# A two-block transformer step on one core: five context tiles put between the second mixer's attention steps, and the memory attention taken in halves

## The reference, cut to what matters

```python
def first_block(x, mem, ...):                     # DEPTH = 2
    mem_n = rmsnorm(mem, mem_norm)
    for i in range(DEPTH):
        h = rmsnorm(x, mix_norm[i])
        ...                                       # memory K and V from mem_n: 4 heads of 64
        # i == 0: gated short convolution; i == 1: stick-breaking attention, 12 heads,
        #         on k_sh, v_sh = kv of rmsnorm(x, kv_norm), taken after layer 0
        y_mem = memory_cross_attention(q_mem, mem_k, mem_v)
        x = x + jnp.concatenate([y_main, y_mem], axis=-1) @ w_o[i]
        x = x + swiglu(rmsnorm(x, ffn_norm[i]), w_gate[i], w_up[i], w_down[i])   # 1024 -> 2816 -> 1024
        ...
    return rmsnorm(x, final_norm)

def _context_states(hc, w_in, gla_w2, gla_b2, s0):
    k, v, lr = _split(hc @ w_in[:, OFF_KVG:], IN_SPLITS[6:])
    _, s_f, s_b = _gla_bidir(None, ..., lr, gla_w2, gla_b2, s0, s0)
    return s_f, s_b

# second_block: modulations = silu(c) @ w_ada + b_ada, and the same of c_ctx
hc = _modulate(_rms_norm(ctx, norm1_g[l]), sh1c, sc1c)
s_f, s_b = _context_states(hc, ...)               # lr 1 tile, k 4 tiles, v 8 tiles of weights
hx = _modulate(_rms_norm(x, norm1_g[l]), sh1x, sc1x)
y_x, _, _ = _token_mixer(hx, *tm, s_f, s_b)       # then a convolutional feed-forward and a last norm
```

## Time and profile before

| | |
|---|---|
| runs | 1208.05, 1209.74, 1212.25 us; median 1209.74 |
| the profiled execution | 1211.49 us; its span 1210.2 us |
| granted TensorE clock over the span | 0.984 |
| PE busy | 1157.9 us (96%) |
| DVE, ACT, POOL busy | 833.1, 622.6, 149.4 us |
| HBM read | 219.42 MB |

### The profile page before, as it was taken

How to read it: one execution, slowest core, us unless ns; L and a number is a source line. 1 busy time by engine, 2 the same in 40 slices (tenths; PEclk the granted TensorE clock), 3 DMA queues, 4 the chain that set the end, 5 groups by cost and what they waited for, 6 DMA issues and landing times.

```text
span 1210.2 us, 21837 instructions
## 1 busy us (share of the span) xinstructions
PE 1157.9 (96%) x9014; PEld 1110.4 (92%) x9014; DVE 833.1 (69%) x1278; ACT 622.6 (51%) x938; POOL 149.4 (12%) x111
## 2 busy tenths in 40 slices
PE   7999999999899899999999999999999989999996
PEld 6999999999788789999998898979899988999995
DVE  5677677778774756877787756577646767677775
ACT  5655444445564645444455664656437444555553
POOL 0003000000100012000000000000001032344431
PEclk9999999999999989999999999999999997999999
DMA  8655587776744144877877445354324552556550
GB/s 310 195 163 178 165 295 253 240 246 229 244 128 136 51 157 146 263 263 252 274 265 232 160 157 166 105 174 140 114 95 158 185 182 90 186 178 192 175 157 36
DMA packets 60467, 221.90 MB, mean 183 GB/s; under 512 B 6752, under 2 KB 7008, under 8 KB 59984
## 3 DMA queue, kind: packets, MB, share of 16 engines
q1 hardware_dynamic: 59904, 219.06, 55.0%
q10 hardware_dynamic: 288, 1.05, 0.2%
q0 software_dynamic: 176, 0.39, 0.1%
HBM read 219.42 MB, written 1.05 MB: 182 GB/s over the span
## 4 chain that ended last, share of the span: by engine, by line
PE 81%; DVE 10%; ACT 5%; issue 3%; DMA 1%; SPq 0%; POOL 0%; ACTq 0%; DVEq 0%
PE PS L350 23%; PE PS L352 22%; PE PS L351 22%; PE PS L355 13%; DVE w_lo L1316 4%; ACT w_hi L837 3%; DVE PS L1889 1%; DVE SQ L1587 1%; DMA ARENA<-memT 1%; DVE raw L1338 0%; DVE SQ L1352 0%; DVE ARENA L1352 0%; PE PS L455 0%; DVE H_lo L1362 0%; ACT ARENA L925 0%
## 5 line engine op out<-in xcount | busy, mean ns | idle before, releaser
L1316 DVE TENSOR_TENSOR w_lo<-raw,w_hi 128x1024 fp32r<-128x1024 f32 x325 | 398.8, 1228 | 259.9 <-ACT w_hi L837 259.4
L837 ACT ACTIVATE w_hi<-raw 128x1024 fp32r<-128x1024 f32 x356 | 372.5, 1054 | 141.7 <-PE PS L352 117.4
L350 PE MATMUL PS<-Y_hi,w_hi 128*128 128x256 f32 x1240 | 358.4, 289 | 9.6 <-DVE w_lo L1316 4.2
L351 PE MATMUL PS<-Y_lo,w_hi 128*128 128x256 f32 x1240 | 353.9, 285 | 0.0
L352 PE MATMUL PS<-Y_hi,w_lo 128*128 128x256 f32 x1240 | 353.8, 285 | 0.0
L350 PEld LDWEIGHTS PS<-Y_hi,w_hi 128*128 128x128 f32 x1240 | 240.8, 194 | 16.2 <-issue 9.4
L351 PEld LDWEIGHTS PS<-Y_lo,w_hi 128*128 128x128 f32 x1240 | 241.2, 194 | 0.4 <-issue 0.2
L352 PEld LDWEIGHTS PS<-Y_hi,w_lo 128*128 128x128 f32 x1240 | 241.0, 194 | 0.0
L350 PE MATMUL PS<-H_hi,w_hi 128*128 128x256 f32 x808 | 232.1, 287 | 5.3 <-DVE w_lo L1316 2.8
L351 PE MATMUL PS<-H_lo,w_hi 128*128 128x256 f32 x808 | 229.3, 284 | 0.0
L352 PE MATMUL PS<-H_hi,w_lo 128*128 128x256 f32 x808 | 229.2, 284 | 0.0
(11 more groups left out here) (206 smaller groups left out, 1316.7 us busy)
## 6 DMA issues: line engine op xcount, KB each, us to landing
raw<-stream SPq DMA_DIRECT2D x404, 512.0 KB, 4.2
ARENA<-memT SPq DMA_DIRECT2D x2, 512.0 KB, 7.7
X<-xT SPq DMA_DIRECT2D x1, 1024.0 KB, 11.4
ARENA<-c_rows SPq DMA_DIRECT2D x2, 512.0 KB, 8.2
ARENA<-memT SPq DMA_DIRECT2D x1, 1024.0 KB, 7.1
ARENA<-ctxT SPq DMA_DIRECT2D x1, 1024.0 KB, 8.1
outT<-ARENA SPq DMA_DIRECT2D x2, 512.0 KB, 2.6
CROW<-c_rows SPq DMA_DIRECT2D x1, 512.0 KB, 10.2
```

The source lines that it names most:

```text
L350: pe.matmul(o, wh, xh, start=start, stop=False, skip_group_check=True)
L351: pe.matmul(o, wh, xl, start=False, stop=False, skip_group_check=True)
L837: act.activation(w_hi[n % RING][:], raw[at][:], ACT.Copy).then_inc(*mark("hi", n))
L1316: dve.tensor_tensor(w_lo[n % RING][:], raw[raw_of("slot", n)][:], w_hi[n % RING][:], ALU.subtract).then_inc(*mark("lo_dve", n))
```

## The change

It does six things.

1. `STAGES`: `ctx_lr` and `ctx_k` (five tiles) move from behind `ffn1` to behind `kv_v1`. They read the context's norm from `CX_hi`, `CX_lo`, new names for the places of `CTX` and `CSQ`.
2. The attention of the second mixer: PE scores the memory heads at step 1 of `b_q` instead of step 7; its two halves of heads wait for their own marks; on ACT and DVE it runs interleaved with the norm for K and V (`both`). It ends on all three engines at step 13, and `stick_schedule` starts there on all three. Before, PE started the groups at step 18 and ACT and DVE at 17.
3. `stick_output` becomes `stick_outputs`, a task beside the groups, at steps 14, 16 and 18 of its own count.
4. The context's squares and norm: `context_rms` moves to `a_u`/`a_b`, `context_norm` to the last six j of `ffn0` behind `memory_norm`; its 1 MB load moves with it, to tile `a_c`+4.
5. The 16 double mods lie in j = 0 to 15 of `ffn0`; `ffn1` has 32 single ones (two for odd j from 3 on). The second load and silu of c_ctx go.
6. `block1_end` has 8 tiles beside it instead of 13, with new steps.

```diff
@@ STAGES, MODS_AFTER
-          ("kv_v1", 2), ("w_o1", KC), ("ffn1", FFN_SLOTS),
-          ("ctx_lr", 1), ("ctx_k", 4), ("ctx_v0", 4), ("ctx_v1", 4),
+          ("kv_v1", 2), ("ctx_lr", 1), ("ctx_k", 4), ("w_o1", KC), ("ffn1", FFN_SLOTS),
+          ("ctx_v0", 4), ("ctx_v1", 4),
...
-    if _j % 2 == 0 and _both < CTX_MODS:
-        _now = [_both]
+    if _l == 0:
+        _now = [_j] if _j < CTX_MODS else []
     else:
-        _now = [CTX_MODS + _one + i for i in range(2 if _l and _j in (11, 13, 15, 17) else 1)]
+        _now = [len(MOD_ORDER) + _i for _i in range(2 if _j % 2 and _j > 2 else 1)]
...
+def both(first, second):
+    live = [first, second]
+    while live:
+        live = [task for task in live if next(task, "end") != "end"]
+        if live:
+            yield
...
@@ PE, memory_attention
                 last.then_inc(*mark("ma_scores", l))
-                for b in bs:
-                    emptied[b] = [("ma_exp", l, 7)]
-                yield from nothing(6)
-                pe.wait_ge(*past("ma_prob", l, 7))
-                claim(*bs)
                 for h in range(MEMH):
+                    emptied[bs[h]] = [("ma_exp", l, 2 * h + 1)]
+                for h in range(MEMH):
+                    if h % 2 == 0:
+                        yield from pace.to(7 + l + h // 2)
+                    pe.wait_ge(*past("ma_prob", l, 2 * h + 1))
+                    claim(bs[h])
                     for mt in range(TT):
...
                 for h in range(MEMH):
+                    if h % 2 == 0:
+                        yield from pace.to(9 + l + h // 2)
+                    if h == 0:
+                        claim(*os)
                     pe.wait_ge(*past("ma_pt", l, h))
...
-                yield
+                yield from pace.to(12 + l)
@@ PE, stick_outputs
-            def stick_output():
+            def stick_outputs():
+                pace = Pace()
                 for c in range(MC):
-                    b = 4 + c // 2
+                    b = 2 + c // 2
                     if c % 2 == 0:
+                        yield from pace.to(14 + c)
                         claim(b)
+                    if c == 0:
+                        pe.wait_ge(*past("vs", 1))
                     pe.wait_ge(*past("am", c))
@@ PE, block1_end
+                pace = Pace()
                 yield
                 quarters("final")
-                yield
-                yield
+                yield from pace.to(2)
                 sum_quarters("final")
-                yield
-                yield from nothing(5)
+                yield from pace.to(6)
                 quarters("norm1")
-                yield
-                yield
+                yield from pace.to(7)
                 sum_quarters("norm1")
-                yield from nothing(KC + 2)
@@ PE, order of the stages
-            side.tasks += [memory_attention(1), stick_schedule(stick_group, lambda: kept)]
+            side = Side(memory_attention(1), both(stick_schedule(stick_group, lambda: kept), stick_outputs()))
...
+            project("ctx_lr", 1, CX, lambda i: ("lr", 0), side, [norm_low("ctx", k) for k in range(KC)])
+            project("ctx_k", GH, CX, lambda i: ("kb", 0, i), side)
             side.finish()
-            pe.wait_ge(*past("vs", 1))
-            stick_output()
-            side = Side(context_rms())
...
-            project("w_o1", KC, H, lambda i: ("added", 1, i), side, y_ready)
-            side.finish()
-            ffn(1, Side(nothing(KC + 1)))
+            project("w_o1", KC, H, lambda i: ("added", 1, i), None, y_ready, order=(0, 1, 2, 3, 6, 7, 4, 5))
+            ffn(1)
@@ ACT and DVE, memory_attention(1) beside the norm for K and V
+            side.tasks = [both(memory_attention(1), chain(*side.tasks)),
+                          both(stick_schedule(stick_group, lambda: kept), stick_outputs())]
@@ DVE, memory_attention: maxima and probabilities by halves, at steps 1, 3 and 4
-                dve.tensor_reduce(mx.rearrange("p (h t) -> p h t", h=4), scores, AX,
-                                  ALU.max).then_inc(*mark("ma_max0", l))
...
+                for half in range(2):
+                    hs, cols = slice(2 * half, 2 * half + 2), slice(4 * half, 4 * half + 4)
+                    dve.tensor_reduce(mx[:, cols].rearrange("p (h t) -> p h t", h=2), scores[:, hs], AX,
+                                      ALU.max).then_inc(*mark("ma_max0", l, half))
...
+                for half in range(2):
+                    cols = slice(4 * half, 4 * half + 4)
+                    yield from pace.to(3 + half)
+                    dve.wait_ge(*past("ma_exp", l, 4 * half + 3))
...
@@ DVE, block1_end
+                pace = Pace()
                 add_down(1)
-                yield from nothing(3)
+                yield
+                yield from pace.to(3)
                 dve.wait_ge(*past("rs", "final"))
                 for c in range(KC):
...
-                    if c % 2:
-                        yield
-                yield from nothing(3)
+                    if c == 3:
+                        yield from pace.to(4)
+                yield from pace.to(8)
```

217 lines of the change are left out of this document (99 added, 118 removed).

## The result

The changed kernel takes 1219.92 us in the median of four runs (1218.57 to 1222.87), beside 1210.32 of the kernel before (1208.05 to 1212.25): a ratio of 1.0083 (of the means), with a 95% interval from 1.0057 to 1.0109. It is slower by about 10 us where 1207.5 was forecast, and lies outside the range.

A forecast was written before the change was run, and what follows sets the result against it. PE was taken as the bound, busy 1157.9 of 1210.2 us. Terms -2.9 -3.8 -1.2 -2.7 +6.6 +1.7 = -2.3 took the profiled 1211.5 to 1209.2, about 1207.5 for a median; range 1200.5 to 1214.

The forecast's parts named there:

- the price of the lower clock: Half-clock time after new PE waits of 2 us or more: one new drop net, +1.7 us, between 0 and 5.
- stick groups: Second mixer's attention groups: moved tiles cover part of the chain, new waits remain; -3.8 us, bounds -12.0 and 0.
- memory attention: Memory heads in b_q: earlier scores and halves cut the excess from 5.3 to 2.4 us, so -2.9.
- context's squares: Context's squares and sum, moved earlier: about 2 us of PE in either place, so no change.
- ffn0, ffn1: The feed-forwards with mods and norms rearranged: -1.2 us in the first, -2.7 in the second.
- end of the block: First block's end with eight wide tiles instead of 13: cover taken away, +6.6 us, bounds +0.6 and +8.
- three new long waits: PE waits of 2 us or more: before group 5's tails, the second quarters and inside the lr tile.
- The slower rival: Many short and three long waits bring the lower clock repeatedly: five drops, +6.8 us, 1214.3 us; chance 0.16.
- Sum 8.2: New loss in the attention groups: waits before tails of groups 1 to 5 and z of groups 0 and 1, us.
- old 12.0: Excess in us of the kernel before, from 409.36 to 439.92, the end of w_o1's first tile.
- masks in time: Attention groups: tiles cover the chain, none of the 8.2 us of waits comes back, 1199.3 us; chance 0.12.
- norms in time: First block's end: its two waits (2.9 and 3.2 us) don't show, 1201.4 us; chance 0.12.

The follow-up runs named there:

- halves alone: The kernel before with only the memory attention by halves, scores six steps earlier; groups, tiles, mods and context norm stay where they were: 1207.88 us, ratio 0.9974.
- wait made on purpose: The kernel with the groups and block's end both repaired, plus six POOL operations that PE must await at chunk 6 of lr: 1207.09 us, ratio 0.9962.
- the block's end made sooner: The changed kernel with the steps of the first block's end laid for eight tiles, x_final, squares and norm sooner: 1210.49 us, ratio 0.9994.
- more matmuls: The changed kernel with extra unread matmuls (8, 4, 9 and 18) ahead of four waits between 667 and 702 us: 1217.98 us, ratio 1.0050.
- the repair: The changed kernel with ACT and DVE one step ahead of PE in every attention group, as in the kernel before: 1208.97 us, ratio 0.9978.
- the two repairs: The changed kernel with ACT and DVE one step ahead in the groups and the block's end laid for eight tiles: 1197.25 us, ratio 0.9878.

## Why the prediction was wrong

Two terms of the sum carry most of the miss: the price of the lower clock (+1.7, and +5.5 came) and the gain of the stick groups (-3.8, and -0.6 came). Each line below is a term, as predicted and as the profiled executions show it. They stand for 7.1 of the 9.6 us between the medians: the changed kernel's profiled execution was its fastest, with a granted clock of 0.987 where the other three have 0.983 or 0.984, and no trace shows where those lost more.

| term | predicted | measured | how |
|---|---|---|---|
| memory attention | -2.9 | -2.9 | halves alone: 46.41 to 43.49 |
| stick groups | -3.8 | -0.6 | 122.90 to 117.0 is -5.9; less 2.9 and the 2.4 of the context's squares that left w_o1 (22.51 - 7 x 2.88) |
| ffn0, ffn1 | -1.2, -2.7 | -0.9, -1.4 | 197.14 to 196.22, 193.56 to 192.14; in ffn0 only 0.3 is the change's: the kernel with the halves alone, which lacks the low row at 133.44, has 196.54 |
| context's squares | 0 | +0.7 | a_b 17.28 to 20.39, less the 2.4 |
| end of the block | +6.6 | +7.8 | 30.5 to 38.69, less 0.4 that the clock took in lr (38.30 without) |
| clock | +1.7 | +5.5 | k 3.5, lr 0.4, vs0 1.6 |
| start | 0 | -1.1 | mem_k0 21.30 to 20.19; 19.7 to 21.6 in the experiments, whose edits don't touch it |
| sum | -2.3 | +7.1 | profiled: 1218.57 - 1211.49 = 7.1 |

**The clock, "I take one new drop net: +1.7".** This term is off most, by 3.8 us, though 1.6 of it lies at vs0, where a low stretch comes and goes between kernels. Of the three new long waits two came (2.47 and 2.64); the third was 1.22. And one drop of the clock followed the wait in lr, as forecast. The price was wrong: I took it from a row of 3.41 us at half clock, and the wait in lr was followed by 10.24, or by 6.83 in two experiments; k and lr paid 3.9. The wait made on purpose confirms it from outside: 3.29 us cost 7.6 in lr and k. The slower rival had five drops, 8.5 us in all, brought by the many short waits; what came was 5.5 from two places.

The prediction weighed the Trainium skill there (TensorE: Matmul & The Clock Gate, HAM oscillation and the second failure mode: frequent small idles make the clock swing). The traces do not agree with it here: the crowded stretch 340.62 to 472.03, with all its waits, has a granted clock of 1.00, while one wait of 3.03 us among full tiles brought a low row. They contradict it only in part: in two other kernels with the same steps (the block's end made sooner, more matmuls) a row of 3.41 us at half clock stands behind the wait of 2.5 us ahead of the last tails, at 432 and 433. The same page of the Trainium skill (Why this matters for your kernels) warns of single long pauses between bursts of matmuls, but only of pauses longer than this one. The traces agree that a single wait can do it, and not with that limit: 10.24 us at half clock followed 2.64 us of waiting.

**The groups, "Sum 8.2" of an "old 12.0".** This was the step I had called most sure, and it is off by 3.2 us. The mechanism, the place and the waits were right; the sizes were not. The stretch that gained most when the new waits were undone was this one, 10.3 us. I had priced each wait by its length, and a group pays more: 1.64 us for a wait of 1.38. The seven waits that the repair removed (six ahead of tails, 0.25, 1.38, 1.26, 1.26, 1.17 and 2.47, and 0.98 ahead of a z) add up to 8.8 and cost 10.3. That is 2.1 of the 3.2. The other 1.1 is the old excess, which I had put at 12.0: with these waits gone the groups are only 10.9 us better than before (0.6 + 10.3). In it are w_o1's eight tiles, which take 24.05 us behind the last outputs where 23.04 were foreseen. Measured against the kernel with the halves alone, whose groups are 1.1 us shorter than before, the changed kernel's groups gained nothing.

**ffn1.** 1.0 of the 1.3 missed is the bank order of w_o1, which I had read over in the diff: its eighth tile lands in bank 0, which ffn1's first tile claims.

**The end of the block.** Both waits came. The one ahead of the second quarters was 1.22 and then slow pacing (four quarters of 0.63 with 0.17 between), instead of one of 2.9; lr's was 2.64 with smaller ones. Together 1.2 more than the sum.

**Context's squares.** They were costed at nothing, as "about 2 us of PE in either place". It is 2.4 in w_o1 and 3.1 in a_b: there PE idles 0.4 for them.

Of the rivals, "masks in time" and "norms in time" did not happen by themselves, but the two repairs made them happen, and 0.9878 shows what the change could bring: 14.8 us under the kernel before, 12 of them without moving a tile, as said above. Forecast for both together in my terms: 1207.5 - 8.2 - 6.1 = 1193.2, less the clock's 1.7 = 1191.5; measured 0.9878 x 1210.3 = 1195.5.

What stays open: why vs0's stage has a low stretch in some kernels and not in others, with the same wait of 2.57 us in it; what sets the length of a low stretch, with 10.24 and 6.83 us behind the same wait of 2.64; and where the changed kernel's slower executions lost their time.

## What to carry to other kernels

Tiles put beside a chain of small steps cover it only if every engine's step stands a tile ahead of its reader: here five tiles bought 2.2 us out of step, 4.8 in step, and three then did the same for that stretch. Weigh what the tiles leave behind: 7.4 us, until the steps there were laid anew. Where tiles are taken away, lay the steps of what stays anew for the smaller number; that alone was worth 10 us. And a wait is not priced by its bracket: measure from one repeated instruction to the next, and look at the granted clock of the stage behind it.

## What the runs showed of the hardware that was not expected

- The price of one PE wait: 1.00 us in lr cost 1.2; 3.29 there cost 7.6 in lr and k, 10.2 by the ratios; 3.03 among full tiles cost 4.7. The stretches at half clock behind them were none, 10.24 and 3.41 us long. The price is not fixed by the wait: behind 2.64 us in lr 10.24 us at half clock came once and 6.83 twice, behind about 1 us none came twice and 3.41 once.
- Matmuls added to fill the waits did not keep the clock up: with 18 the low stretch was 3.41 us long (10.24 and 6.83 without them), with 39 it stayed 3.41 and another of 3.41 began among the added ones.
- Low stretches in stages that an edit doesn't touch come and go between kernels: ffn2 takes 205.0 to 205.2 us in nine of the seventeen kernels, 202.3 in three and 203.7 to 204.2 in the rest, vs0 14.6 or about 16. Single profiled executions differ by 3 us for this alone, so a term under that is better read from its stage than from the total.
